# Banded attention: the rotary partners of queries and keys exchanged by VectorE in 32-partition instructions, in place of TensorE swap products

## The chip, the cores and the metric

The kernel runs on one core of a Trainium2 chip. The metric is the device time of one execution in microseconds (us), as the median over several runs. Five engines work side by side and meet at semaphores: TensorE (PE; its weight loads are listed as PEld), VectorE (DVE), ScalarE (ACT), GpSimd (POOL) and SyncE (SP), which issues the DMAs.

## What is computed

The program computes three transformer layers in float32 over 512 tokens. The change lies in the third, in its sliding-window attention: 16 query heads and 2 key/value heads of 64 features, each query seeing 128 positions. Before the scores, queries and keys pass through a rotary embedding:

```python
def rotary(x, pos):
    d = x.shape[-1]; half = d // 2
    ...
    x1, x2 = xf[..., :half], xf[..., half:]
    out = jnp.concatenate([x1 * cos - x2 * sin, x2 * cos + x1 * sin], axis=-1)

aq = rotary(aq.reshape(B, S, ATTN_Q_HEADS, ATTN_HEAD_DIM), pos)
ak = rotary(ak.reshape(B, S, ATTN_KV_HEADS, ATTN_HEAD_DIM), pos)
ay = sliding_window_sink_attention(aq, ak, av, attn_sinks)   # softmax over a band, with a sink
```

Here `d` is 64, so every feature has its partner 32 features away.

## The kernel before

Activations lie with the features on the 128 partitions and the 512 tokens along the free dimension, so that a tile of 128 partitions holds two heads: partitions 0 to 63 are one head, 64 to 127 the other, and the rotary partner of a feature is 32 partitions up or down. A tile such as `qk`, `kq` or `kks` (128 x 2 x 512) holds two such blocks, four heads.

Weights arrive as slabs of 1 MB (`raw`). ACT rounds a slab to its high part (`split_hi`, L362), DVE takes the difference (`split_lo`, L366), and PE multiplies each block in three products (high by low, low by high, high by high): L301 to L303 in `product`, L2817 to L2819 in `swa_steps`. One such product of 512 columns is what the program calls a matmul here; a slab has 48.

The attention stage has two parts. `kv_pe`, `kv_act` and `kv_dve` make the values, rotate the keys and the first queries, and run four products of slabs. Then `swa_pe`, `swa_act` and `swa_dve` run four rounds j = 0 to 3, each for four query heads and with four units v = 0 to 3. The order on each engine is written out by hand. On PE, `scores` (L2852), `turn` (transposes of the probabilities, L2863) and `values` (L2880) are set in between steps of `fill`, which are slices of nine slab products that have nothing to do with the attention of that round; one `fill` step is three matmuls. On DVE each round is: `maxima` and `norms` for the units, two `split_lo`, and at the end of the round `queries_dve(j + 1)`, the rotation of the next round's queries. On ACT: exponentials, the evictions of slab products (`out`, which writes `qk`, `mg` or `it`), `turned`, `split_hi`.

The rotation (`rope_dve`) is three DVE instructions of 128 x 1024: the cosine product (L2477), the sine product (L2478), which reads the exchanged partners from PSUM, and the sum (L2479). The partners are exchanged by PE: a product of the tile with a permutation matrix `swp`, two instructions of 512 columns in float32, shown in the trace as four matmuls. There are five: for the keys (`swap_keys`, L2735), for the first queries (`swap_first`, L2741) and, inside the rounds 0, 1 and 2, for the queries of the next round (`swap`, L2838), after `turn(j, 2)` and one `fill` step, and ahead of `values(j, 2)`. The semaphore `sw` tells DVE that they are done. `scores(j + 1, 0)` waits for `qr`, which the last DVE instruction of the rotation raises. At the end of a round the orders are:

```python
# PE, round j                      # DVE, round j
turn(j, 2)                         norms(j, 2)
fill(1)                            split_lo(dve, Slab(G_SWA + 2 * j + 2))
swap(j + 1)   # only if j < 3      norms(j, 3)           # raises pn
fill(2); values(j, 2); fill(3)     queries_dve(dve, chain, j + 1)   # raises qr
turn(j, 3)    # waits for pn       maxima(j + 1, 0)      # waits for sc
fill(2); values(j, 3)
scores(j + 1, 0)   # waits for qr, raises sc
```

`chain.link` makes DVE wait for the instruction just issued before it starts the next. In `rope_dve` only the step from L2478 to L2479 is linked so.

Of the kernel before, what the change touches and what calls it, by code (L numbers as in the profile page):

```python
# [15 lines left out]
P = 128  # L16
DM, T, NT = 1024, 512, 4
KC = DM // P
# [20 lines left out]
G_KV = G_RET + N_RET  # L39
G_AQ = G_KV + N_KV  # L40
G_RO = G_AQ + 1
# [78 lines left out]
def build(nc, slabs, ada, vecs, consts, masks, rope, vbias, pos, xin, out):  # L120
    fp32, f32r, i32 = mybir.dt.float32, mybir.dt.float32r, mybir.dt.int32
    ALU, ACT, AX = mybir.AluOpType, mybir.ActivationFunctionType, mybir.AxisListType
    V_, S_, T_ = nc.vector, nc.scalar, nc.tensor
    ctx = ExitStack()
    with ctx:
# [3 lines left out]
        def sem(name):  # L129
            return ctx.enter_context(nc.semaphore(name))  # L130
# [158 lines left out]
        def product(pe, s, kc, nt, H, L, between={}):  # L289


            pe.wait_ge(lo_ready, s.plus(1))
            if s.b >= 2:
                pe.wait_ge(bank_free[s.slot], s.prior())
            for m in range(nt):
                for k in range(kc):
                    if m * kc + k in between:
                        between[m * kc + k]()
                    w = slice((k * nt + m) * P, (k * nt + m + 1) * P)
                    o = D[s.slot][:, m, :]  # L300
                    T_.matmul(o, lo[s.slot][:, w], H[:, k, :], start=(k == 0), stop=False)  # L301
                    T_.matmul(o, hi[s.slot][:, w], L[:, k, :], start=False, stop=False)  # L302
                    last = T_.matmul(o, hi[s.slot][:, w], H[:, k, :], start=False, stop=(k == kc - 1))  # L303
            last.then_inc(slab_done, 1)
# [2164 lines left out]
                                          "rs", "o", "H", "L")}  # L2469
        HS = 3  # L2470
        b_col = lambda o, i=None, step=0: vec[:, bass.ds(at(V["b_in"] + o, i, step), 1)]
        pairs = lambda ap: ap.unsqueeze(1).to_broadcast([P, 2, T])

        def rope_dve(chain, dst, raw_, cos_, sin_, swapped=None, tmp=None):

            swapped, tmp = (D[2], tm2) if swapped is None else (swapped, tmp)
            V_.tensor_tensor(dst[:], raw_[:], pairs(cos_), ALU.mult)  # L2477
            chain.link(V_.tensor_tensor(tmp[:], swapped[:], pairs(sin_), ALU.mult))  # L2478
            return V_.tensor_tensor(dst[:], dst[:], tmp[:], ALU.add)  # L2479

        def ret_pe(pe):
            def body(i):
# [181 lines left out]
        def merge_dve(dve, chain, base, hb):  # L2666
# [37 lines left out]
            for m in range(2):  # L2704
# [2 lines left out]
            split_lo(dve, Slab(base + 9))  # L2707


        as_ = {n: sem("a_" + n) for n in ("sw", "kk", "hb", "qr", "sc", "sb", "mx", "ex", "pn", "tr", "pt", "pv", "H", "L",  # L2710
                                         "half_done", "half_free", "ga")}
        kks, av, ptb = rg, rvt, ka
        two_rows = lambda c: tab[:, c * T:(c + 2) * T].rearrange("p (a n) -> p a n", a=2)
# [5 lines left out]
        AU = 4  # L2719
# [10 lines left out]
        def kv_pe(pe):  # L2730
            k = Slab(G_KV)

            def swap_keys():
                for e in range(2):
                    last = T_.matmul(D[2][:, e, :], swp[:, 0:P], qk[:, e, :], start=True, stop=True)  # L2735
                last.then_inc(as_["sw"], 1)

            def swap_first():
                pe.wait_ge(bank_free[Slab(G_AQ).slot], Slab(G_AQ).prior(1))
                for e in range(2):  # L2740
                    last = T_.matmul(D[3][:, e, :], swp[:, 0:P], qk[:, e, :], start=True, stop=True)  # L2741
                last.then_inc(as_["sw"], 1)
            product_t(pe, k.next(), KC, hH, hL, P)
            product(pe, Slab(G_AQ), KC, 2, hH, hL, {4: swap_keys})
            pe.wait_ge(rs_["L"], 4)
            product(pe, Slab(G_RO), KC, 2, rH, rL, {6: swap_first})
            product(pe, Slab(G_RO + 1), KC, 2, rH, rL)
            product(pe, Slab(G_RO + 2), KC, 2, rH, rL)

# [15 lines left out]

        def queries_dve(dve, chain, j):

            dve.wait_ge(as_["sw"], j + 2)
            rope_dve(chain, kq, qk, acos, asin, D[3], rtm).then_inc(as_["qr"], 1)

        def kv_dve(dve, chain):
            v = Slab(G_KV + 1)
            split_lo(dve, Slab(G_AQ))
            dve.wait_ge(slab_done, v.plus(1))
            V_.tensor_tensor(av[:, :, 0:P], D[v.slot].rearrange("p a (b n) -> p (a b) n", b=2)[:, :, 0:P],
                             vb[:, 8 * P:9 * P].unsqueeze(1).to_broadcast([P, NT, P]),
                             ALU.add).then_inc(bank_free[v.slot], 1)
            split_lo(dve, Slab(G_RO))
            dve.wait_ge(as_["sw"], 1)
            rope_dve(chain, kks, qk, acos, asin).then_inc(as_["kk"], 1)  # L2780
            V_.tensor_scalar(half_b, vec[:, V["b_in"] + 16:V["b_in"] + 24], 0.5, None, ALU.mult).then_inc(as_["hb"], 1)
            split_lo(dve, Slab(G_RO + 1))
            queries_dve(dve, chain, 0)
            split_lo(dve, Slab(G_RO + 2))
            split_lo(dve, Slab(G_SWA))
# [38 lines left out]
        def swa_pe(pe):  # L2824
            w = lambda n, k: pe.wait_ge(as_[n], k)
            ahead = swa_steps(pe)

            def fill(n):
                for _ in range(n):
                    next(ahead)  # L2830

            def swap(j):
                q = 2 * j - 2
                for m in range(2):
                    half_free(pe, q, m)
                w("sb", AU * j)
                for e in range(2):
                    last = T_.matmul(D[3][:, e, :], swp[:, 0:P], qk[:, e, :], start=True, stop=True)  # L2838
                last.then_inc(as_["sw"], 1)

            def scores(j, v):
                if v:
                    w("sb", AU * j + v)
                else:
                    w("qr", j + 1)
                m, bp = divmod(v, 2)
                for e in range(2):
                    b = 2 * bp + e
                    k0 = max(b - 1, 0) * P
                    for hh in range(2):  # L2850
                        half = slice(64 * hh, 64 * hh + 64)
                        last = T_.matmul(four(D[3])[:, 2 * hh + e, :], kq[half, m, b * P:b * P + P],  # L2852
                                         kks[half, j // 2, k0:k0 + 2 * P], start=True, stop=True)
                last.then_inc(as_["sc"], 1)

            def turn(j, v):
                u = AU * j + v
                w("pn", u + 1)
                if u:
                    w("pt", u)  # L2860
                for b in range(NT):
                    for k in range(2):
                        last = T_.transpose(four(D[2])[:, b, k * P:k * P + P],  # L2863
                                            four(prb[v % 2])[:, b, k * P:k * P + P], ident)
                last.then_inc(as_["tr"], 1)

            def values(j, v):
                w("pt", AU * j + v + 1)
                if v == 0:
                    if j:  # L2870
                        w("L", j)
                    else:
                        pe.wait_ge(bank_free[1], Slab(G_RO + 2).prior(1))
                m, bp = divmod(v, 2)
                for e in range(2):
                    b = 2 * bp + e
                    k0 = max(b - 1, 0)
                    for k in range(2 if b else 1):
                        for hh in range(2):
                            last = T_.matmul(D[1][64 * hh:64 * hh + 64, m, b * P:b * P + P],  # L2880
                                             av[:, k0 + k, 64 * (j // 2):64 * (j // 2) + 64],
                                             four(ptb)[:, 2 * hh + e, k * P:k * P + P],
                                             start=(k == 0), stop=(k == (1 if b else 0)))
                last.then_inc(as_["pv"], 1)
            w("kk", 1)
            for j in range(AJ):
                scores(j, 0)
                fill(3)
                scores(j, 1)
                fill(7)  # L2890
                turn(j, 0)
                fill(1)
                scores(j, 2)
                fill(3)
                values(j, 0)
                fill(4)
                turn(j, 1)
                fill(1)
                scores(j, 3)
                fill(2)  # L2900
                values(j, 1)
                fill(3)
                turn(j, 2)
                fill(1)
                if j + 1 < AJ:
                    swap(j + 1)
                fill(2)
                values(j, 2)
                fill(3)
                turn(j, 3)  # L2910
                fill(2)
                values(j, 3)
            fill(2 * KC)
            w("L", AJ)
# [522 lines left out]
```

## Time and profile before

| what | value |
|---|---|
| time, median of 3 runs | 2376.18 us (2374.58 to 2378.06) |
| the profiled execution | 2376.76 us |
| its span, first to last instruction | 2374.9 us |
| mean granted TensorE clock | 0.995 of full speed |
| busy over the span | PE 97%, PEld 80%, DVE 56%, ACT 39%, POOL 16% |
| chain of work that ended last | PE 72%, POOL 10%, issue 6%, DVE 5%, ACT 3% |

How to read it: the span is the profiled execution's own time without launch and end. The chain is followed back from the last instruction, at each step to what released it. A busy PE is only the sum of its matmuls as shown; which wait ends last at one point is read from the timeline there. The stage that the change touches runs from about 1655 to 1860 us.

### The profile page before, as it was taken

What the parts mean: (1) busy time and instruction counts of PE and PEld (TensorE: products, weight loads), DVE (VectorE), ACT (ScalarE), POOL (GpSimd) and SP (SyncE); (2) the same over time, 40 slices, a digit from 0 to 9 for tenths busy, and PEclk for the clock granted to TensorE, in tenths of its full rate; (3) what the DMA queues carried; (4) which work ended last, traced back from release to release, by engine and by line L of the source; (5) the groups of instructions that cost most, each with busy time, mean ns of one, the idle gap of its engine ahead of it and who ended that gap; (6) DMA issues with size and microseconds to landing.
All of it is one profiled execution on the core that took longest, in us unless ns stands there. A gap on an engine that the chain in (4) does not pass through costs nothing.

```text
span 2374.9 us, 32501 instructions
## 1 busy us (share of the span) xinstructions
PE 2301.6 (97%) x13527; PEld 1900.8 (80%) x13527; DVE 1334.2 (56%) x1657; ACT 936.0 (39%) x1275; POOL 371.0 (16%) x164
## 2 busy tenths in 40 slices
PE   6999999999999999999999999999999999999998
PEld 4677878888878886668888888888777788898887
DVE  4766755542376565547763466434367345864365
ACT  4546553442313354434332235344255324332232
POOL 0346456357780000000000000000000000000000
PEclk9999999999999999999999999999999999999999
DMA  7433232334442324311333232211211222223232
GB/s 298 141 113 137 107 116 90 124 142 177 185 187 87 110 76 155 124 54 71 107 104 109 90 112 106 89 53 71 89 54 56 87 89 76 103 102 111 89 107 89
DMA packets 40749, 260.40 MB, mean 110 GB/s; under 512 B 4432, under 2 KB 6832, under 8 KB 10416
## 3 DMA queue, kind: packets, MB, share of 16 engines
q1 hardware_dynamic: 40624, 258.59, 30.2%
q8 instruction: 96, 1.57, 0.3%
q14 instruction: 29, 0.24, 0.0%
HBM read 256.42 MB, written 2.15 MB: 109 GB/s over the span
## 4 chain that ended last, share of the span: by engine, by line
PE 72%; POOL 10%; issue 6%; DVE 5%; ACT 3%; DMA 1%; POOLq 0%; DVEq 0%; ACTq 0%
PE D L301 8%; PE D L302 8%; PE D L303 8%; POOL adar L375 6%; POOL adar L373 5%; PE D L1626 3%; PE D L1625 3%; PE D L1624 3%; PE D L1663 3%; PE D L1661 3%; PE D L1662 3%; PE D L2817 2%; PE D L1399 1%; PE D L2819 1%; PE D L2818 1%
## 5 line engine op out<-in xcount | busy, mean ns | idle before, releaser
L366 DVE TENSOR_TENSOR lo<-raw,hi 128x2048 fp32r<-128x2048 f32 (+3 forms) x136 | 300.9, 2213 | 202.4 <-ACT hi L362 202.3
L362 ACT ACTIVATE hi<-raw 128x2048 fp32r<-128x2048 f32 (+3 forms) x136 | 239.7, 1762 | 365.4 <-PE D L303 267.9
L301 PE MATMUL D<-hH,lo 128*128 128x512 f32 x640 | 258.8, 404 | 5.5 <-DVE lo L366 5.5
L302 PE MATMUL D<-hL,hi 128*128 128x512 f32 x640 | 252.4, 394 | 0.0
L303 PE MATMUL D<-hH,hi 128*128 128x512 f32 x640 | 252.4, 394 | 0.0
L375 POOL TENSOR_TENSOR adar<-adar 128x1024 f32<-128x1024 f32 (+2 forms) x120 | 215.0, 1791 | 9.4
L373 POOL TENSOR_TENSOR adar<-adar,small 128x2048 f32<-128x2048 f32 x40 | 156.6, 3915 | 322.6 <-DVE zi L1285 187.3
L301 PE MATMUL D<-aH,lo 128*128 128x512 f32 x390 | 155.1, 398 | 0.0
L302 PE MATMUL D<-aL,hi 128*128 128x512 f32 x390 | 154.6, 396 | 0.0
L303 PE MATMUL D<-aH,hi 128*128 128x512 f32 x390 | 154.4, 396 | 0.0
L301 PEld LDWEIGHTS D<-hH,lo 128*128 128x128 f32 x640 | 120.6, 188 | 36.1 <-DVE lo L366 7.0
L302 PEld LDWEIGHTS D<-hL,hi 128*128 128x128 f32 x640 | 120.6, 188 | 29.1 <-issue 2.4
L303 PEld LDWEIGHTS D<-hH,hi 128*128 128x128 f32 x640 | 120.5, 188 | 28.2
L1663 PE MATMUL D<-hH,hi 128*128 128x512 f32 x304 | 120.1, 395 | 0.0
L1662 PE MATMUL D<-hL,hi 128*128 128x512 f32 x304 | 120.0, 395 | 0.0
L1661 PE MATMUL D<-hH,lo 128*128 128x512 f32 x304 | 120.0, 395 | 0.0
L1399 PE MATMUL D<-hH,lo 128*128 128x512 f32 x240 | 107.6, 448 | 2.4 <-DVE vs L1178 2.2
L1625 PE MATMUL D<-tL,hi 128*128 128x256 f32 x384 | 108.1, 282 | 0.0
L1626 PE MATMUL D<-tH,hi 128*128 128x256 f32 x384 | 108.1, 281 | 0.0
L1624 PE MATMUL D<-tH,lo 128*128 128x256 f32 x384 | 108.1, 281 | 0.0
L557 DVE SCALAR_TENSOR_TENSOR x<-D,mod,x 128x512 f32<-128x512 f32 (+1 forms) x40 | 28.9, 747 | 124.1 <-PE D L303 107.7
L1401 PE MATMUL D<-hH,hi 128*128 128x512 f32 x240 | 94.8, 395 | 0.0
(544 smaller groups left out, 5506.0 us busy)
## 6 DMA issues: line engine op xcount, KB each, us to landing
raw<-in_slabs SPq DMA_DIRECT2D x185, 1024.0 KB, 4.8
adar<-in_ada SPq DMA_DIRECT2D x42, 1024.0 KB, 4.8
fw<-in_ada SPq DMA_DIRECT2D x6, 1024.0 KB, 22.8
x<-in_xin SPq DMA_DIRECT2D x2, 1024.0 KB, 9.0
dt<-bcast SPq DMA_DIRECT2D x8, 256.0 KB, 3.3
dtb<-bcast SPq DMA_DIRECT2D x8, 256.0 KB, 3.5
qd<-bcast SPq DMA_DIRECT2D x8, 256.0 KB, 3.8
out<-x SPq DMA_DIRECT2D x8, 256.0 KB, 2.2
```

The source lines that it names most:

```text
L301: T_.matmul(o, lo[s.slot][:, w], H[:, k, :], start=(k == 0), stop=False)
L302: T_.matmul(o, hi[s.slot][:, w], L[:, k, :], start=False, stop=False)
L303: last = T_.matmul(o, hi[s.slot][:, w], H[:, k, :], start=False, stop=(k == kc - 1))
L362: S_.activation(hi[s.slot][:, 0:n], raw[s.slot][:, 0:n], ACT.Copy).then_inc(hi_ready, 1)
L366: V_.tensor_tensor(lo[s.slot][:, 0:n], raw[s.slot][:, 0:n], hi[s.slot][:, 0:n], ALU.subtract).then_inc(lo_ready, 1)
L373: chain.link(nc.gpsimd.tensor_tensor(r3, r3, cact.unsqueeze(2).to_broadcast([P, KC, 2 * P]), ALU.mult))
L375: last = nc.gpsimd.tensor_tensor(r3[:, 0:n], r3[:, 0:n], r3[:, n:2 * n], ALU.add)
L1624: T_.matmul(to, w(lo, k), H(k), start=(k == 0), stop=False)
L1625: T_.matmul(to, w(hi, k), L(k), start=False, stop=False)
L1661: T_.matmul(to, lo[x][:, w], hH[:, k, :], start=(k == 0), stop=False)
L1662: T_.matmul(to, hi[x][:, w], hL[:, k, :], start=False, stop=False)
L1663: last = T_.matmul(to, hi[x][:, w], hH[:, k, :], start=False, stop=(k == KC - 1))
```

## The change

`rope_parts` takes the place of `rope_dve` for the five rotations of this stage (the retention stage ahead of it keeps `rope_dve` and its own swap products at L2492). The sine product is taken straight from SBUF, in four DVE instructions of 32 partitions x 1024 that read one quarter of the partitions and write the quarter beside it; each of them is followed by a wait for itself (`chain.link`). The last instruction subtracts instead of adding, because the sine table is now read at the source partition, where its sign is the other one. All five swap products and the semaphore `sw` are gone, and DVE waits for what the swap products had waited for. The keys' rotation uses `tm2` as its scratch tile, the queries' `rtm`, as before.

```diff
--- before.py
+++ after.py
@@ -2469,7 +2469,7 @@
                                           "rs", "o", "H", "L")}
         HS = 3
         b_col = lambda o, i=None, step=0: vec[:, bass.ds(at(V["b_in"] + o, i, step), 1)]
-        pairs = lambda ap: ap.unsqueeze(1).to_broadcast([P, 2, T])
+        pairs = lambda ap: ap.unsqueeze(1).to_broadcast([ap.shape[0], 2, T])
 
         def rope_dve(chain, dst, raw_, cos_, sin_, swapped=None, tmp=None):
 
@@ -2479,6 +2479,14 @@
             return V_.tensor_tensor(dst[:], dst[:], tmp[:], ALU.add)
 
 
+
+        def rope_parts(chain, n, dst, raw_, cos_, sin_, tmp):
+
+            V_.tensor_tensor(dst[:], raw_[:], pairs(cos_), ALU.mult)
+            for a in range(0, P, 2 * n):
+                for to, of in ((a, a + n), (a + n, a)):
+                    chain.link(V_.tensor_tensor(tmp[to:to + n], raw_[of:of + n], pairs(sin_[of:of + n, :])[:], ALU.mult))
+            return V_.tensor_tensor(dst[:], dst[:], tmp[:], ALU.subtract)
 
         def ret_pe(pe):
             def body(i):
@@ -2707,7 +2715,7 @@
             split_lo(dve, Slab(base + 9))
 
 
-        as_ = {n: sem("a_" + n) for n in ("sw", "kk", "hb", "qr", "sc", "sb", "mx", "ex", "pn", "tr", "pt", "pv", "H", "L",
+        as_ = {n: sem("a_" + n) for n in ("kk", "hb", "qr", "sc", "sb", "mx", "ex", "pn", "tr", "pt", "pv", "H", "L",
                                          "half_done", "half_free", "ga")}
         kks, av, ptb = rg, rvt, ka
         two_rows = lambda c: tab[:, c * T:(c + 2) * T].rearrange("p (a n) -> p a n", a=2)
@@ -2730,20 +2738,10 @@
         def kv_pe(pe):
             k = Slab(G_KV)
 
-            def swap_keys():
-                for e in range(2):
-                    last = T_.matmul(D[2][:, e, :], swp[:, 0:P], qk[:, e, :], start=True, stop=True)
-                last.then_inc(as_["sw"], 1)
-
-            def swap_first():
-                pe.wait_ge(bank_free[Slab(G_AQ).slot], Slab(G_AQ).prior(1))
-                for e in range(2):
-                    last = T_.matmul(D[3][:, e, :], swp[:, 0:P], qk[:, e, :], start=True, stop=True)
-                last.then_inc(as_["sw"], 1)
             product_t(pe, k.next(), KC, hH, hL, P)
-            product(pe, Slab(G_AQ), KC, 2, hH, hL, {4: swap_keys})
+            product(pe, Slab(G_AQ), KC, 2, hH, hL)
             pe.wait_ge(rs_["L"], 4)
-            product(pe, Slab(G_RO), KC, 2, rH, rL, {6: swap_first})
+            product(pe, Slab(G_RO), KC, 2, rH, rL)
             product(pe, Slab(G_RO + 1), KC, 2, rH, rL)
             product(pe, Slab(G_RO + 2), KC, 2, rH, rL)
 
@@ -2765,8 +2763,13 @@
 
         def queries_dve(dve, chain, j):
 
-            dve.wait_ge(as_["sw"], j + 2)
-            rope_dve(chain, kq, qk, acos, asin, D[3], rtm).then_inc(as_["qr"], 1)
+            if j:
+                for m in range(2):
+                    half_free(dve, 2 * j - 2, m)
+                dve.wait_ge(as_["sc"], AU * j)
+            else:
+                dve.wait_ge(bank_free[Slab(G_AQ).slot], Slab(G_AQ).prior(1))
+            rope_parts(chain, P // 4, kq, qk, acos, asin, rtm).then_inc(as_["qr"], 1)
 
         def kv_dve(dve, chain):
             v = Slab(G_KV + 1)
@@ -2776,8 +2779,9 @@
                              vb[:, 8 * P:9 * P].unsqueeze(1).to_broadcast([P, NT, P]),
                              ALU.add).then_inc(bank_free[v.slot], 1)
             split_lo(dve, Slab(G_RO))
-            dve.wait_ge(as_["sw"], 1)
-            rope_dve(chain, kks, qk, acos, asin).then_inc(as_["kk"], 1)
+            k = Slab(G_KV)
+            dve.wait_ge(bank_free[k.slot], k.prior(1))
+            rope_parts(chain, P // 4, kks, qk, acos, asin, tm2).then_inc(as_["kk"], 1)
             V_.tensor_scalar(half_b, vec[:, V["b_in"] + 16:V["b_in"] + 24], 0.5, None, ALU.mult).then_inc(as_["hb"], 1)
             split_lo(dve, Slab(G_RO + 1))
             queries_dve(dve, chain, 0)
@@ -2828,15 +2832,6 @@
             def fill(n):
                 for _ in range(n):
                     next(ahead)
-
-            def swap(j):
-                q = 2 * j - 2
-                for m in range(2):
-                    half_free(pe, q, m)
-                w("sb", AU * j)
-                for e in range(2):
-                    last = T_.matmul(D[3][:, e, :], swp[:, 0:P], qk[:, e, :], start=True, stop=True)
-                last.then_inc(as_["sw"], 1)
 
             def scores(j, v):
                 if v:
@@ -2902,8 +2897,6 @@
                 fill(3)
                 turn(j, 2)
                 fill(1)
-                if j + 1 < AJ:
-                    swap(j + 1)
                 fill(2)
                 values(j, 2)
                 fill(3)
```

## Rows read from the trace of the kernel before

**Rows 1.** The page: the span, and busy time by engine (share, instructions).

```profile
span 2374.9 us, 32501 instructions
...
PE 2301.6 (97%) x13527; PEld 1900.8 (80%) x13527; DVE 1334.2 (56%) x1657; ACT 936.0 (39%) x1275; POOL 371.0 (16%) x164
```

**Rows 2.** Windows of both parts: length, busy and count by engine, clock, DMA, GB/s.

```profile
1655.00:1715.00 60.00, 60.00 (x303) 49.35 (x301) 23.36 (x18) 15.49 (x14) 0.00 (x0) 1.00 0.26 88
1715.00:1860.00 145.00, 144.29 (x848) 105.57 (x846) 101.01 (x134) 78.12 (x186) 0.00 (x0) 1.00 0.15 51
```

**Rows 3.** The chain that ended last, 1655 to 1850 us: start, length, what.

```profile
1670.05 1.72 PE D L2735 x4
...
1742.91 1.72 PE D L2838 x4
...
1752.42 1.06 PE D L2852 x8
```

**Rows 4.** Line L2838 alone: matmuls of the three swaps in the rounds, ns.

```profile
L2838 PE MATMUL D<-qk,swp x12: 591/592/592, 1742.8 to 1818.6; 128*128 128x512 f32 x12
```

**Rows 5.** Timeline, end of round 0, DVE: start, length, instruction, idle before it.

```profile
1744.87 2.29 DVE L366 TENSOR_TENSOR lo<-raw,hi 128x2048 fp32r<-128x2048 f32 x1 [4.21 <-ACT hi L362]
...
1747.49 1.23 DVE L3006 TENSOR_TENSOR tab<-tab,small 128x1024 f32<-128x1024 f32 x1
...
1748.63 1.22 DVE L2477 TENSOR_TENSOR kq<-qk,tab 128x1024 f32<-128x1024 f32 x1
...
1749.76 1.22 DVE L2478 TENSOR_TENSOR tab<-D,tab 128x1024 f32<-128x1024 f32 x1
...
1751.02 1.23 DVE L2479 TENSOR_TENSOR kq<-kq,tab 128x1024 f32<-128x1024 f32 x1
```

**Rows 6.** Timeline, the same stretch, ACT.

```profile
1742.02 1.03 ACT L2952 ACTIVATE ka<-D 128x1024 f32<-128x1024 f32 x1
...
1742.94 1.90 ACT L362 ACTIVATE hi<-raw 128x2048 fp32r<-128x2048 f32 x1
```

**Rows 7.** Timeline, weight loads of PE: the end of round 0, then one in round 1.

```profile
1748.76 0.99 PEld L2863 LDWEIGHTS D<-cst,tab 128*128 128x128 f32 x8
...
1752.34 0.73 PEld L2852 LDWEIGHTS D<-rg,kq 64*128 64x128 f32 x8 [0.17 <-DVE kq L2479]
...
1761.91 0.86 PEld L2863 LDWEIGHTS D<-cst,rsq 128*128 128x128 f32 x8 [0.44 <-DVE rsq L3006]
```

**Rows 8.** Timeline, DVE in the first part, keys and first queries.

```profile
1671.81 1.23 DVE L2477 TENSOR_TENSOR rg<-qk,tab 128x1024 f32<-128x1024 f32 x1 [0.25 <-PE D L2735]
...
1683.27 2.29 DVE L366 TENSOR_TENSOR lo<-raw,hi 128x2048 fp32r<-128x2048 f32 x1 [7.76 <-ACT hi L362]
1686.09 1.23 DVE L2477 TENSOR_TENSOR kq<-qk,tab 128x1024 f32<-128x1024 f32 x1 [0.52 <-PE D L2741]
...
1695.92 2.29 DVE L366 TENSOR_TENSOR lo<-raw,hi 128x2048 fp32r<-128x2048 f32 x1 [6.21 <-ACT hi L362]
```

**Rows 9.** Timeline, ACT in the first part: the eviction that waits for the keys.

```profile
1680.17 1.27 ACT L2757 ACTIVATE qk<-D,vec 128x512 f32<-128x512 f32 x2 [10.94 <-PE D L303]
```

**Rows 10.** DVE groups by form: names, shapes, count, busy us, mean ns, idle.

```profile
L1338 DVE TENSOR_TENSOR go<-go,vT 128x1024 f32<-128x1024 f32 x3 | 4.7, 1569 | 0.0
...
L366 DVE TENSOR_TENSOR lo<-raw,hi 128x384 fp32r<-128x384 f32 x4 | 2.2, 558 | 3.4 <-ACT hi L362 3.4
...
L908 DVE COPY go<-D 32x384 f32<-32x384 f32 x1 | 0.5, 539 | 0.0
```

**Rows 11.** Windows, columns as in Rows 2: PE gaps elsewhere and what follows.

```profile
701.10:703.40 2.30, 0.00 (x0) 0.00 (x0) 2.27 (x2) 1.91 (x1) 2.12 (x2) 1.00 0.70 196
704.00:707.30 3.30, 3.30 (x9) 2.61 (x9) 3.30 (x4) 0.00 (x0) 0.00 (x0) 0.50 0.25 104
...
1043.00:1044.80 1.80, 0.00 (x0) 0.00 (x0) 1.22 (x3) 0.52 (x2) 0.00 (x0) 1.00 0.00 0
1045.40:1048.60 3.20, 3.20 (x13) 2.81 (x12) 0.00 (x0) 0.60 (x1) 0.00 (x0) 0.50 0.00 0
```

## The prediction

> **What bounds the kernel now.** I read the page first: PE is busy for 97% of the span, DVE for 56% [rows 1]. Then the windows of the two parts of the stage: from 1655 to 1715 us PE has no idle time at all, in the rounds 144.29 of 145.00 us are busy, and DVE is busy for 101.01 of them [rows 2]. So PE sets the pace. The chain of waits agrees: through the whole stage it runs over PE's matmuls, and each exchange of partners stands in it as a piece of 1.72 us [rows 3]. All of them run at full clock, with the same length every time [rows 4]. Read like this alone, taking five pieces of 1.72 us off PE is a gain of 8.6 us. The average hides one thing, though, which the timeline at the end of a round shows: there DVE is as late as PE.
>
> Follow DVE at the end of round 0 [rows 5]. It waits 4.21 us for ACT's `split_hi`, takes 2.29 us for `split_lo`, then normalises unit 3 (L3006, to 1748.72), then rotates the queries in three instructions, the last from 1751.02 to 1752.25. PE loads the first weights of `turn(0, 3)` at 1748.76, right after the normalisation ends, and those of `scores(1, 0)` at 1752.34, after a wait of 0.17 us for the rotation [rows 7]. Both of PE's steps are thus at DVE's heels already, before anything is added.
>
> **What is removed.** Five exchanges of 1.72 us on PE, 8.6 us in all. Where does each go?
>
> The first two lie in the first part. There nothing else is near: DVE waits 7.76 and 6.21 us ahead of its `split_lo` [rows 8], PE for nobody [rows 2]. DVE loses its own short waits for the exchanges, 0.25 and 0.52 us [rows 8]. These two exchanges are a clean gain, 2 x 1.72 = 3.4 us, if the longer rotations stay hidden (next part).
>
> The three in the rounds lie after `turn(j, 2)` and ahead of `turn(j, 3)`. What PE waits for at `turn(j, 3)` is fixed by other engines: ACT turns unit 2 (to 1743.05), rounds the slab (to 1744.84) [rows 6], DVE subtracts and normalises to 1748.72 [rows 5]. All that ACT and DVE need for it was made by PE ahead of the exchange. So without the exchange PE comes to `turn(j, 3)` 1.72 us sooner and waits there for the same instant, give or take 0.1 us. The three exchanges in the rounds give nothing; only the place of the time changes, from a matmul to a wait.
>
> **What is added.** In each rotation one DVE instruction of 128 x 1024 (L2478, 1.22 us) becomes four of 32 x 1024. The trace has no such instruction, so its price has to be bounded. From below, if time went with the partitions: from 558 ns for 128 x 384 [rows 10] to 1.22 us for 128 x 1024 [rows 5] it is 1.04 ns for each element of a partition, so 1.07 us of the 1.22 goes with the data and 0.15 us is fixed; a quarter of the partitions would then take 0.27 + 0.15 = 0.42 us. But the only 32-partition row, a copy of 32 x 384 from PSUM, takes 539 ns, against 558 ns for 128 x 384 [rows 10]: the time goes with the free dimension alone. From above: there are rows of 128 x 1024 at 1569 ns on average (L1338) [rows 10], from a stage in which POOL works as well; here POOL does nothing [rows 2]. I take 1.22 us, the value of the same operands at full height. Each of the four waits for itself; the one linked step of before, L2478 to L2479, goes from start to start in 1751.02 - 1749.76 = 1.26 us [rows 5]. So four linked steps take 5.04 us where one took 1.26, and `qr` comes 3 x 1.26 = 3.8 us later after the cosine product has begun.
>
> The Trainium skill has a rule that speaks against this part of the change ("VectorE: DVE Perf Modes", Rules for kernel authors): since every DVE instruction drains anyway, it is the number of instructions that should be small. By its formula for a float32 tensor_tensor, (N + 151)/0.96 ns, one part is an estimate of 1224 ns, which the rows of full height agree with. Another section, Two Vector instructions with no wait between them, says that an instruction whose input starts in another group of 32 partitions than the last one's begins only when its forerunners have ended. By that the first part would start 1.26 instead of 1.13 us after the cosine product, 0.1 us more for each rotation and 0.4 us for the three in the rounds; no row of before shows it, and I leave it out of the sum.
>
> *Keys and first queries.* DVE starts the keys at 1671.6 (no exchange to wait for) and ends 1.13 + 4 x 1.26 + 1.23 = 7.4 us later, at 1679.0. ACT's eviction over the keys' raw tile began at 1680.17 when PE's product ended [rows 9]; that product ends 1.72 us sooner, at about 1678.4, so ACT is held for 0.6 us or so. What follows (ACT's rounding, DVE's `split_lo`, 2.29 us) is done by about 1684.6, and PE needs it only when the slab product in between, of 11.2 us (48 matmuls of some 0.233 us), ends at about 1689.6. Likewise the first queries: from about 1684.6 to 1692.0, when the next `split_lo`, which in before started at 1695.92 [rows 8], can start at about 1692.5. Both extra 3.8 us are hidden under slab products, at nothing. If that cover were gone they would cost up to 3.8 us each.
>
> *The rounds.* Here there is no cover. DVE begins the cosine product at 1748.63 as before, since what DVE newly waits for is older: in ACT's order both halves of `qk` are written ahead of the `turned` that starts at 1742.02 [rows 6], and the round's last scores are older still (their unit is what `norms(0, 3)` normalises at 1747.49 [rows 5]). Nothing queued behind that wait on DVE is held by it. It ends 3.8 us later. PE has come to `scores(j + 1, 0)` when it did before, as `turn(j, 3)` holds it, and had waited 0.17 us [rows 7]; now it stands for about 4.0 us. PE has nothing else to do: its order is written out and the next `fill` lies behind the scores. Behind PE's scores come DVE's `maxima`, ACT's exponentials and all of round j + 1, so that the delay isn't made up. Three times 3.8 us is 11.3 us.
>
> *The clock.* A gap of 4 us on PE has a second price. Elsewhere in this trace, after PE had stood for 2.30 us, the granted clock was 0.50 (1.2 instead of 2.4 GHz) for the next 3.3 us, while PE worked all the time; after a gap of 1.80 us it was the same for 3.2 us [rows 11]. Each such stretch costs half its length, about 1.7 us. The three gaps to come are longer than either. Against the full price: part of a low stretch may fall into the gap itself, and DVE is the later one by 0.44 us at the first `turn` of round 1 [rows 7], so that much of PE's slowness is free. I take 1.2 us each, between ends of 0 and 1.7: 3.6 us.
>
> **The sum.** -3.4 + 11.3 + 3.6 = +11.5 us. The profiled execution took 2376.76 us, 0.6 us above the median of the runs; on the median the sum gives 2376.18 + 11.5 = 2387.7 us.
>
> **The rivals.**
> *Stalls without the low clock:* the same waits, but the clock stays full, or the low stretch falls into the gap. -3.4 + 11.3 = +7.9 us, 2384.1 us. Against it stand both pairs of [rows 11].
> *DVE stays hidden, PE is all that counts (faster):* this is the reading of the page, PE at 97% and DVE at 56%. It would give -8.6 us, 2367.6 us. It needs `turn(j, 3)` not to be held by DVE and the four parts together to be no longer than the one they replace, 0.3 us each; [rows 5] and [rows 7] speak against both.
> *The parts cost by their partitions (no change):* 0.42 us and 0.04 us for the link, four times, is 1.84 us against 1.26, so `qr` comes 0.6 us later, three times 1.7 us, too short for the clock: -3.4 + 1.7 = -1.7 us, 2374.5 us. The sign turns where `qr` is 1.15 us late, at 0.6 us for a part. Only the 32 x 384 row speaks on it, and against it.
> *Parts that move data across partitions are dearer* than rows of full height: at 1.57 us each, `qr` is 4 x 0.35 = 1.4 us later still, 4.2 us in all, 2391.9 us. No row shows a shift of partitions, which is why it keeps a chance.
> A page of the Trainium skill bears on the last two: the "Vector Engine (DVE) Microarchitecture Reference" calls moves from one group of 32 partitions to another free. No run so far shows it.
>
> **How the numbers follow.** The forecast, stalls with the low clock, has 0.72; stalls without it 0.12; dearer parts 0.07; price by partitions 0.05; DVE hidden 0.04. A measurement can tell about 0.2%, 4.8 us, from no change. The first three are slower: 0.91. Price by partitions is no change: 0.05. DVE hidden is faster: 0.04. The range takes in the clock's ends (0 and 1.7 us each, +7.9 to +13.0 us), some 0.4 us for each end's small unknowns, and part of the dearer case: 2383.5 to 2391.0 us.
>
> **What the profile of after would show.** Right: no line with `swp` in this stage; four DVE instructions of 32 x 1024 in a row at about 1.22 us, starts 1.26 us apart; PE waiting about 4 us for the subtraction three times, 1.5 us for the normalisation ahead of `turn(j, 3)` three times; the first part 3.4 us shorter, the rounds 15 us longer; 0.50 in the clock column after each long gap. Wrong: parts of about 0.4 us (then price by partitions); PE's long wait absent (then my claim about who is late at the round's end falls); a first part that isn't shorter (then the keys' rotation holds ACT and PE); no 0.50 (then 2384).

## The result, and the profile after

| | before | after |
|---|---|---|
| median of the runs | 2376.64 us (2374.58 to 2378.06, 4 runs) | 2391.11 us (2390.86 to 2392.19, 4 runs) |
| profiled execution's span | 2374.9 us | 2389.9 us |
| ratio to before, 95% interval | | 1.0062 [1.005, 1.0074] |

The change makes the kernel 14.5 us slower, 0.6%. The forecast was +11.5 us, with a range up to 2391.0: right in sign, and the time lies 0.1 us beyond the range.

The page of after, busy time by engine as in [rows 1]:

```profile
span 2389.9 us, 32476 instructions
PE 2303.6 (96%) x13507; PEld 1903.3 (80%) x13507; DVE 1354.1 (57%) x1672; ACT 936.4 (39%) x1275; POOL 369.3 (15%) x164
```

PE has 20 matmuls fewer and is busy for 2 us more: that alone says that some of its work ran slower. Windows of the stage, columns as in [rows 2]:

```profile
1655.00:1712.00 57.00, 57.00 (x296) 48.23 (x296) 30.64 (x24) 16.26 (x14) 0.00 (x0) 1.00 0.27 93
1712.00:1875.00 163.00, 146.57 (x837) 107.84 (x835) 112.67 (x143) 78.23 (x186) 0.00 (x0) 0.95 0.13 46
```

In the first part PE is still never idle. In the rounds it now stands for 16.4 us, where it had stood for 0.7, and the granted clock is 0.95. The chain of waits at the end of round 0, which in before ran over PE alone [rows 3], now runs over DVE (start, length, what):

```profile
1742.20 2.29 DVE lo L366
...
1745.96 1.22 DVE kq L2485
...
1747.19 1.22 DVE tab L2488
...
1748.44 1.23 DVE tab L2488
...
1749.69 1.23 DVE tab L2488
...
1750.94 1.23 DVE tab L2488
...
1752.19 1.24 DVE kq L2489
...
1753.47 2.08 PE D L2847 x8
```

L2488 is the new line of the four products. They start 1.25 us apart. The last row is the first scores of round 1: 2.08 us for what took 1.06 in before [rows 3], at half the clock. The weight loads of PE there, which answer to [rows 7]:

```profile
1746.09 0.86 PEld L2858 LDWEIGHTS D<-cst,tab 128*128 128x128 f32 x8 [1.79 <-DVE tab L2999]
...
1753.47 1.36 PEld L2847 LDWEIGHTS D<-rg,kq 64*128 64x128 f32 x8 [4.10 <-DVE kq L2489]
```

and the sum of these waits in the rounds (total us, times, longest). Of the four at the last `turn`, the one of round 3 stands in the kernel before too, with the same 1.8 us:

```profile
PEld D L2847 <- DVE kq L2489: 12.3, 3, 4.1
...
PEld D L2858 <- DVE tab L2999: 7.2, 4, 1.8
```

Where the time went can be read off by following the same DVE instruction in both traces; only the difference of its starts counts:

| instruction (line in before) | before, us | after, us | lag |
|---|---|---|---|
| last step of the retention stage (L2610) | 1655.88 | 1656.63 | +0.75 |
| `split_lo` after the first queries (L366) | 1695.92 | 1693.23 | -2.69 |
| subtraction for the queries of round 1 (L2479) | 1751.02 | 1752.19 | +1.17 |
| third `maxima` of round 1 (L2987) | 1764.81 | 1768.52 | +3.71 |
| subtraction for round 2 (L2479) | 1788.31 | 1795.86 | +7.55 |
| fourth `maxima` of round 2 (L2990) | 1810.85 | 1819.70 | +8.85 |
| subtraction for round 3 (L2479) | 1825.62 | 1838.33 | +12.71 |
| fourth `maxima` of round 3 (L2990) | 1848.14 | 1863.06 | +14.92 |

The steps: -3.44 us for the first part; +3.86, +3.84 and +3.86 from the rotations, 11.56 in all; +2.54, +1.30 and +2.21 behind them, 6.05 in all; and 0.75 us that had arisen before the stage began, where nothing was changed (1.2 us of lag in the first 100 us of the kernel, of which some was made up later). The granted clock belongs to the third kind. Windows of after (columns as in [rows 11]): the first gap, what follows it, and the stretches of the other two gaps:

```profile
1749.70:1752.70 3.00, 0.00 (x0) 0.00 (x0) 2.93 (x3) 2.78 (x2) 0.00 (x0) 1.00 0.00 0
1753.00:1759.40 6.40, 5.93 (x17) 3.99 (x17) 4.12 (x6) 0.90 (x3) 0.00 (x0) 0.50 0.00 1
1760.00:1763.00 3.00, 3.00 (x18) 2.25 (x15) 2.17 (x2) 0.68 (x4) 0.00 (x0) 1.00 0.03 5
1797.30:1800.40 3.10, 3.10 (x11) 2.10 (x12) 1.16 (x1) 0.00 (x0) 0.00 (x0) 0.50 0.00 0
1838.40:1844.80 6.40, 5.19 (x16) 3.69 (x17) 4.12 (x6) 0.38 (x2) 0.00 (x0) 0.50 0.00 0
```

Two of the three low stretches are about 6.8 us long, one is 3.4 us. All rows of the kernel before that the forecast had used were of the short kind [rows 11].

### The profile page after: what moved, and what is told of

Read it like the earlier page. It is cut to its first block, busy times and chain, and to the rows that moved or that the text cites. A ratio compares the mean times of both kernels' runs of the same rounds, so it can differ in the third digit from the quotient of the medians.

```text
span 2389.9 us, 32476 instructions
## 1 busy us (share of the span) xinstructions
PE 2303.6 (96%) x13507; PEld 1903.3 (80%) x13507; DVE 1354.1 (57%) x1672; ACT 936.4 (39%) x1275; POOL 369.3 (15%) x164
## 3 DMA queue, kind: packets, MB, share of 16 engines
q8 instruction: 96, 1.57, 0.3%
## 4 chain that ended last, share of the span: by engine, by line
PE 70%; POOL 10%; issue 6%; DVE 6%; ACT 3%; DMA 1%; POOLq 0%; DVEq 0%; ACTq 0%
PE D L301 8%; PE D L303 8%; PE D L302 8%; POOL adar L375 6%; POOL adar L373 5%; PE D L1624 3%; PE D L1626 3%; PE D L1625 3%; PE D L1663 3%; PE D L1662 3%; PE D L1661 3%; PE D L1399 1%; PE D L2821 1%; DVE lo L366 1%; PE D L1401 1%
## 5 line engine op out<-in xcount | busy, mean ns | idle before, releaser
L366 DVE TENSOR_TENSOR lo<-raw,hi 128x2048 fp32r<-128x2048 f32 (+3 forms) x136 | 300.4, 2209 | 191.8 <-ACT hi L362 191.7
```

Source lines behind the costliest of these rows:

```text
L366: V_.tensor_tensor(lo[s.slot][:, 0:n], raw[s.slot][:, 0:n], hi[s.slot][:, 0:n], ALU.subtract).then_inc(lo_ready, 1)
```

## The experiments

The theory (A in all that follows): the first part gains its two exchanges; in the rounds three waits for DVE count in full, the exchanges taken off PE give nothing, and the rest of the loss is the clock that the long waits lower. Times beside each run are against the kernel before on the same chip, whose medians were 2376.49 us (runs 1 to 4, 25 executions) and 2376.40 us (runs 5 to 8, 19 executions). These and the 2376.64 us of the result agree within 0.3 us, so the runs can be set beside the changed kernel's 2391.11 us too.

**1. The change in the first part alone.**

```diff
 # before.py, with rope_parts added
-            product(pe, Slab(G_AQ), KC, 2, hH, hL, {4: swap_keys})
+            product(pe, Slab(G_AQ), KC, 2, hH, hL)
-            product(pe, Slab(G_RO), KC, 2, rH, rL, {6: swap_first})
+            product(pe, Slab(G_RO), KC, 2, rH, rL)
 # kv_dve: keys by rope_parts; queries_dve:
+            if j:
+                dve.wait_ge(as_["sw"], j)
+                rope_dve(chain, kq, qk, acos, asin, D[3], rtm).then_inc(as_["qr"], 1)
+            else:
+                dve.wait_ge(bank_free[Slab(G_AQ).slot], Slab(G_AQ).prior(1))
+                rope_parts(chain, P // 4, kq, qk, acos, asin, rtm).then_inc(as_["qr"], 1)
```

> The change is made for the keys and the first queries alone; the three rounds keep their swap products and the three-instruction rotation. Theory A (two exchanges of 1.72 us come off PE, their longer rotations are hidden, the whole loss of the change lies in the rounds): 3.4 us less than the kernel before, about 2373.2 us, and no wait of PE before 1712 us. Rival B (the first part isn't hidden either, some of the loss comes from the keys' rotation holding ACT and PE): no gain or a loss, 2376.6 us or more.

Measured: 2373.02 us (10 runs), ratio 0.9981 [0.9971, 0.9991], which is -3.5 us. In its trace the same DVE instructions gain 3.44 us between L2610 and the `split_lo` of 1695.92, and nothing changes from there to the end of the stage. Theory A holds for the first part, rival B falls. This is a faster kernel than both.

**2. The change in the rounds alone.**

```diff
 # before.py, with rope_parts added; queries_dve:
+            if j:
+                for m in range(2):
+                    half_free(dve, 2 * j - 2, m)
+                dve.wait_ge(as_["sc"], AU * j)
+                rope_parts(chain, P // 4, kq, qk, acos, asin, rtm).then_inc(as_["qr"], 1)
+            else:
+                dve.wait_ge(as_["sw"], 2)
+                rope_dve(chain, kq, qk, acos, asin, D[3], rtm).then_inc(as_["qr"], 1)
 # swa_pe
-                if j + 1 < AJ:
-                    swap(j + 1)
```

> The change is made in the three rounds alone; keys and first queries keep their swap products. Theory A: the three waits of 3.86 us for the rotation come in full, 11.6 us, the low clock behind them adds 4 to 6 us, and the exchanges taken off PE give nothing: 15.5 to 18 us more than before, 2392 to 2394.5 us. Rival B (the exchanges in the rounds do give their 5.2 us, and the loss has another place): 10 to 13 us more.

Measured: 2394.75 us (4 runs), ratio 1.0075 [1.0058, 1.0092], +18.3 us, 0.25 us more than the upper end expected; two of its three low stretches were of 6.8 us. The two halves of the change add up: -3.5 + 18.3 = +14.8, against 14.5 measured for the whole. The three exchanges off PE, 5.2 us of its work, bought nothing.

**3. Two of four products in the rounds.** This kernel leaves out the sine products of partitions 64 to 127 for the queries of rounds 1 to 3, so its result is not the layer's; only its time is used.

```diff
-        def rope_parts(chain, n, dst, raw_, cos_, sin_, tmp):
+        def rope_parts(chain, n, dst, raw_, cos_, sin_, tmp, up=P):
-            for a in range(0, P, 2 * n):
+            for a in range(0, up, 2 * n):
-            rope_parts(chain, P // 4, kq, qk, acos, asin, rtm).then_inc(as_["qr"], 1)
+            rope_parts(chain, P // 4, kq, qk, acos, asin, rtm, P // 2 if j else P).then_inc(as_["qr"], 1)
```

> As the changed kernel, but in the rounds the queries' rotation issues only two of its four 32-partition products: the sine products of partitions 64 to 127 are left out for the queries of rounds 1 to 3. The rotation is then 1.25 us longer than in the kernel before instead of 3.86. Theory A (each wait of PE counts in full, and only a long gap lowers the clock): PE waits about 1.6 us instead of 4.1, the clock stays at 1.00, and the time is -3.4 + 3 x 1.35 = +0.6 us against before, about 2377 us. Rival B (the 6 us beyond the waits don't come from the length of the gap but from the three rotations as such): 2383 us.

Measured: 2377.15 us (10 runs), ratio 1.0 [0.9991, 1.001], +0.7 us. The waits, and the window of the rounds:

```profile
PEld D L2847 <- DVE kq L2489: 4.8, 3, 1.6
...
1712.00:1860.00 148.00, 139.34 (x834) 102.63 (x830) 104.70 (x137) 77.74 (x186) 0.00 (x0) 1.00 0.15 50
```

Against the changed kernel 3 x 2.5 = 7.5 us of DVE are gone, but 14.0 us of time. The difference of 6.5 us went with the clock, which stays at 1.00. Rival B (2383 us) falls.

**4. PE kept at work in the gap.** Two blocks of the old swap products, whose result nobody reads, ahead of the first scores of rounds 1 to 3.

```diff
             for j in range(AJ):
+                if j:
+                    w("sb", AU * j)
+                    for _ in range(2):
+                        for e in range(2):
+                            T_.matmul(D[3][:, e, :], swp[:, 0:P], kks[:, e, :], start=True, stop=True)
                 scores(j, 0)
```

> As the changed kernel, but ahead of the first scores of rounds 1 to 3 PE runs two blocks of swap products (2 x 1.72 us) whose result nobody uses, so that it works while it would wait. Theory A (the 6 us beyond the waits are the lowered clock): the wait of PE falls from 4.1 to about 0.6 us, the granted clock stays 1.00 through the rounds, nothing is later than in the changed kernel, and the time falls by 5 to 6 us although PE has 10.3 us more work: about 2385.5 us. Rival B (the clock is harmless, something else costs the 6 us): 2391 us, as the changed kernel.

Measured: 2384.07 us (10 runs), ratio 1.0032 [1.0023, 1.0042], +7.6 us, so 7.0 us less than the changed kernel (5 to 6 expected), with six blocks of 1.72 us more work on PE, 10.3 us. Matmuls at the end of round 0, and the window of the rounds:

```profile
1747.40 3.70 PE L2886 MATMUL D<-rg,swp 128*128 128x512 f32 x8
1751.33 1.14 PE L2847 MATMUL D<-rg,kq 64*128 64x256 f32 x8 [0.23 <-DVE kq L2489]
...
1712.00:1865.00 153.00, 148.24 (x847) 105.92 (x846) 110.40 (x140) 76.62 (x185) 0.00 (x0) 1.00 0.14 49
```

The scores are back at 1.14 us, and DVE's part of the loss is left bare: from one subtraction to the next the lag grows by 3.81 and 3.79 us and by nothing else. This separates the two prices of a wait: 11.5 us for being late, 6 to 7 us for having stood still.

**5. The gap half filled.** As 4 with `range(1)`.

> As the changed kernel, with one block of unused swap products (1.72 us) instead of two ahead of the first scores of rounds 1 to 3, so that PE stands for about 2.3 us. Theory A (gaps of PE lower the clock, and the longer the gap the more of it): gaps of 1.8 and 2.3 us lowered it in the kernel before, so here it falls after some or all of the three, in stretches of 3.4 us rather than 6.8: 2384 us with none, up to 5 us more with all, I expect 2387. Rival B (only that PE has some work in the gap counts, not its length): 2384 us, clock 1.00 throughout the rounds.

Measured: 2385.26 us (4 runs), ratio 1.0045 [1.0028, 1.0062], +8.9 us. I was wrong here: PE stood three times for 1.95 us, and the clock stayed at 1.00 (the gap of round 0, then what follows):

```profile
1749.20:1751.00 1.80, 0.00 (x0) 0.00 (x0) 1.77 (x2) 0.92 (x1) 0.00 (x0) 1.00 0.00 0
1751.20:1755.00 3.80, 3.80 (x21) 2.71 (x23) 2.61 (x3) 0.00 (x0) 0.00 (x0) 1.00 0.02 4
```

In its trace the stage costs the same as in run 4. The 1.2 us between the medians of 4 and 5 is inside their intervals. Yet the windows of 1.80 and 2.30 us in [rows 11] were followed by a low clock in the kernel before. They lie inside gaps that, from the end of one matmul to the start of the next, are 1.94 and 2.35 us long, so that the shorter one is as long as those of this run. The same gap near 1043 us stands in this run's trace too, and here nothing followed it:

```profile
1042.60:1044.40 1.80, 0.00 (x0) 0.00 (x0) 1.22 (x3) 0.52 (x2) 0.00 (x0) 1.00 0.03 9
1044.60:1048.00 3.40, 3.40 (x24) 3.04 (x24) 0.00 (x0) 0.60 (x1) 0.00 (x0) 1.00 0.00 0
```

Of the ten traces (both kernels and eight runs) six have a low clock behind this gap and four have none; a gap of 1.53 us near 1020 us is followed by a low clock in six as well. So around 2 us the length of the gap alone doesn't decide; at 3.8 us all nine gaps seen (three each in the changed kernel and in runs 2 and 6) lowered it.

**6. One wait instead of four.**

```diff
                 for to, of in ((a, a + n), (a + n, a)):
-                    chain.link(V_.tensor_tensor(tmp[to:to + n], raw_[of:of + n], pairs(sin_[of:of + n, :])[:], ALU.mult))
+                    last = V_.tensor_tensor(tmp[to:to + n], raw_[of:of + n], pairs(sin_[of:of + n, :])[:], ALU.mult)
+            chain.link(last)
```

> As the changed kernel, but DVE waits for itself only after the last of the four 32-partition products, not after each. If an instruction that starts in another group of 32 partitions than its forerunner is held until that has ended, four of them still take 4 x 1.23 us and the rotation is at most 0.1 us shorter; if they overlap like the unlinked instructions of full height (1.13 us from start to start), it is 0.35 us shorter, and the rounds 1 us. I expect the former: 2391 us.

Measured: 2392.19 us (one run). The four products in round 0, linked (the changed kernel, first row) and with one link (this run, second row):

```profile
1747.19 4.97 DVE L2488 TENSOR_TENSOR tab<-qk,tab 32x1024 f32<-32x1024 f32 x4
```

```profile
1747.52 4.90 DVE L2488 TENSOR_TENSOR tab<-qk,tab 32x1024 f32<-32x1024 f32 x4
```

Without the waits they still start 1.23 us apart and don't overlap, unlike unlinked instructions of full height at 1.13 us [rows 5]. The four waits for itself cost 0.07 us together; it is the number of instructions that costs. This is the rule of the Trainium skill ("VectorE: DVE Perf Modes", Two Vector instructions with no wait between them) that the prediction had left out of its sum, and the trace agrees with it. No run has 32-partition products that stay in one group, so whether the change of group holds them or their height of 32 is not shown.

**7. The same work in another order.** In the changed kernel DVE waits 4.22 us for ACT's rounding, as in [rows 5], with the next queries already there. This run uses that gap.

```diff
-                split_lo(dve, Slab(G_SWA + 2 * j + 2))
                 norms(j, 3)
                 if j + 1 < AJ:
                     queries_dve(dve, chain, j + 1)
-                else:
+                split_lo(dve, Slab(G_SWA + 2 * j + 2))
+                if j + 1 == AJ:
                     gate(2)
```

> As the changed kernel, but at the end of rounds 0 to 2 DVE normalises unit 3 and rotates the next queries ahead of the split of the slab, in the 4.2 us in which it waits for ACT's rounding; work and instructions are the same. Theory A (the loss is only that DVE is last at the end of a round): DVE ends the rotation at about 1747.7 on the changed kernel's scale, when PE comes to the first scores without having been held at the last turn; then PE waits about 1.2 us for the split of the slab. That is 0.5 to 0.7 us less than before for each round: 3.4 + 2 = 5.4 us less than the kernel before, 2371 us, with the clock at 1.00. Rival B (the four products cost what they cost wherever they stand, because the split that is now later holds PE instead): 2380 us or more.

Measured: 2370.04 us (10 runs), ratio 0.9975 [0.9965, 0.9984]: -6.4 us against before and 21 us less than the changed kernel, with the same instructions. DVE and the weight loads of PE at the end of round 0:

```profile
1739.53 1.22 DVE L2485 TENSOR_TENSOR kq<-qk,tab 128x1024 f32<-128x1024 f32 x1
1740.76 4.97 DVE L2488 TENSOR_TENSOR tab<-qk,tab 32x1024 f32<-32x1024 f32 x4
1745.77 1.23 DVE L2489 TENSOR_TENSOR kq<-kq,tab 128x1024 f32<-128x1024 f32 x1
1746.91 2.29 DVE L366 TENSOR_TENSOR lo<-raw,hi 128x2048 fp32r<-128x2048 f32 x1
```

```profile
1743.63 1.02 PEld L2858 LDWEIGHTS D<-cst,tab 128*128 128x128 f32 x8
...
1747.23 0.73 PEld L2847 LDWEIGHTS D<-rg,kq 64*128 64x128 f32 x8 [0.17 <-DVE kq L2489]
1749.25 0.19 PEld L2821 LDWEIGHTS D<-hH,lo 128*128 128x128 f32 x1 [1.29 <-DVE lo L366]
```

The last `turn` no longer waits, the scores wait 0.17 us as in [rows 7], and what is late now is the slab's split, by 1.29 us: the next bound, as expected. Each of the rounds 0 to 2 is 1.0 us shorter than before, where I had put 0.5 to 0.7. I had overlooked round 3: it has no queries to rotate, but its last `turn` waited for the same normalisation in the kernel before, and the new order takes that wait away, another 1.54 us by DVE's starts. First part, three rounds and this make 8.0 us in the traces, where the profiled executions are 7.4 us apart and the medians 6.4; that difference stays open. Rival B falls: where the four products stand decides, not that they are there.

**8. The order, with the swap products kept in the rounds.** Run 1 with the order of run 7.

> The changed rotation for keys and first queries, swap products in the rounds, and DVE's order at the round's end as in the run before. Theory A (in the rounds of the kernel before DVE held PE by no more than 0.2 us, so that with swap products there is little for an order to win): 3.4 us for the first part and 0.2 to 0.4 us for each round, 2372.2 us. Rival B (the order as such is worth as much as in the run before, about 2 us over the changed first part): 2371 us or less.

Measured: 2371.32 us (10 runs), ratio 0.9983 [0.9974, 0.9993], -5.1 us. In the trace the rounds 0 to 2 follow one another exactly as in before (from one round to the next the same DVE instructions lead by 4.61 us, 1.18 us of which come from before the stage), so with swap products the order wins nothing there, as theory A has it: PE works through its list. What it wins lies in round 3, which neither expectation had looked at. The weight loads of the last `turn` there, in run 1 and in this run:

```profile
1856.82 0.85 PEld L2876 LDWEIGHTS D<-cst,tab 128*128 128x128 f32 x8 [1.79 <-DVE tab L3019]
```

```profile
1854.30 1.02 PEld L2876 LDWEIGHTS D<-cst,tab 128*128 128x128 f32 x8
```

Behind it the lead is 6.14 us, 1.53 us more, and that is the difference to run 1 (1.7 us by medians). So the median lies between the two expectations, for a reason that neither had. Against this run, run 7 shows what the three exchanges are worth once DVE isn't last: 1.0 us of 1.72 in each round.

## Why the prediction was wrong in size and right in kind

- *The page's average hides that DVE is late at a round's end:* right. PE at 97% and DVE at 56% [rows 1] would have given -8.6 us. The chain of after runs over DVE there.
- *First part, -3.4 us:* -3.44 in the trace, -3.5 as run 1. The cover was as worked out: ACT's eviction, at 1680.17 in [rows 9], was held by DVE until 1679.79, and nobody waited for that.
- *The exchanges in the rounds give nothing:* right. The wait at the last `turn` that takes their place is 1.79 us by weight loads (expected 1.5).
- *Price of a part, 1.22 us by the row of full height:* right, 1216 ns (median of 16, 1211 to 1222). Neither the bound by partitions (0.42) nor the one from L1338 (1.57) was near. The parts read one group of partitions and wrote the other at the price of full height [rows 5], so the move cost nothing. The Trainium skill calls such moves of a 32-partition instruction free ("Vector Engine (DVE) Microarchitecture Reference", The reshape front-end and per-opcode configuration), and the trace agrees.
- *`qr` 3.8 us later, in full, three times, 11.3 us:* 3.86, 3.84, 3.86, in sum 11.56. The 0.1 us of each that is missing is the held first part: from cosine product to first part it is now 1.23 us, where it was 1.13.
- *The clock, 1.2 us each, between 0 and 1.7:* this is the term that failed. It measured 2.54, 1.30 and 2.21 us, 6.05 in all instead of 3.6. The upper end was wrong, not only the choice. I took the length of a low stretch from rows where it was 3.4 us [rows 11] and made a bound of it, though these followed gaps of 2 us and mine were to be of 4. Two of three stretches were 6.8 us long. The trace of before had one of that length, among no rows of the forecast, near the kernel's start: a window inside a gap of 2.8 us, and the stretch that followed:

```profile
25.00:27.70 2.70, 0.00 (x0) 0.00 (x0) 2.56 (x3) 2.28 (x3) 0.00 (x0) 1.00 1.03 434
28.10:34.90 6.80, 6.03 (x15) 4.25 (x14) 5.35 (x7) 2.06 (x3) 0.00 (x0) 0.50 1.01 420
```

  With 3 x 3.4 us as the upper end the range would have held the time. That the time missed the range by only 0.1 us is chance: this is less than runs of one kernel differ by. The term is mis-sized by 2.45 us whichever side of the end the median fell.
- *The rest,* 0.75 us between the profiled executions, arose before the stage, where the kernels are the same, and is within what runs of one kernel differ by.

What rows show of the low stretches: in the changed kernel and runs 2 and 6 there are nine gaps of 3.8 to 3.9 us. In six of them the clock fell 0.4 to 1.6 us before PE took up work again, and stayed low for 6.8 us. In the other three it fell from 0.3 us before to 0.2 us after PE's start, and stayed low for 3.4 us. Half of the low time outside the gap, less some 0.4 us, is what the round lost: in the changed kernel 6.2, 3.4 and 5.4 us outside give 3.1, 1.7 and 2.7, against 2.5, 1.3 and 2.2 measured. The 0.4 us is the slack at the first `turn` that the prediction had named [rows 7]. Why a fall inside the gap lasts twice as long was not tried, and it is no rule of the trace: the stretch of 6.8 us near the start of the kernel before began 0.4 us after PE had taken up work (with one more pause of PE, of 0.8 us, inside it).

## What to carry to other kernels

Before work is moved from the busiest engine to a half-idle one, look where in the order the receiving engine is last. Here 1.72 us of TensorE work for each round bought nothing, since that engine was held by the other one just behind it; and the same instructions, placed in a wait that VectorE already had, made 21 us of difference. Look at every round of the stage for such a wait: the last one, which the change doesn't touch, had 1.5 us in it. A wait of the matrix engine has two prices, the lateness and the lowered clock behind it; bound the second by half the longest low stretch that the whole trace shows, not by those of a few rows. And VectorE's time goes with the instructions and their free size: a quarter of the partitions costs as much as all.

## What the runs showed of the hardware that was not expected

- After TensorE had stood for 3.8 us, the granted clock was at 1.2 GHz for 3.4 us or for 6.8 us. The forecast's rows had only the shorter kind, though one of 6.8 us stood elsewhere in the trace of the kernel before, and this doubled length made the forecast miss.
- A gap of 1.95 us lowered nothing, three times (run 5), where gaps of 1.94 and 2.35 us had in the kernel before. One and the same gap of 1.94 us was followed by a low clock in six of ten traces: some 2 us can go either way.
- Products that nobody reads made a kernel 7 us faster by keeping the clock up (run 4): 10.3 us of added work on TensorE, in three gaps that had been 3.9 us long.
- Four VectorE instructions on different groups of 32 partitions, with no wait between them, didn't overlap at all (run 6: 1.23 us from start to start at 1.22 us each).
